# Conditioning weights of a two-block network: sums kept in SBUF, summed by transposes, and loads dealt out differently over an unrolled kernel

## The reference

```python
def modulate(h, shift, scale):
    return h * (1 + scale) + shift

def adaln(cond, w_ada, b_ada):
    return jnp.split(jax.nn.silu(cond) @ w_ada + b_ada, ADA_CHUNKS, axis=-1)   # ADA_CHUNKS = 6

# in second_block
m_lat = [m[:, None, :] for m in adaln(c, w_ada[l], b_ada[l])]
m_ctx = adaln(c_ctx, w_ada[l], b_ada[l])
hc = modulate(rms_norm(ctx, norm1_g[l]), m_ctx[0], m_ctx[1])
h = modulate(rms_norm(x, norm1_g[l]), m_lat[0], m_lat[1])
x_new = x + m_lat[2] * merge_branches(oa, ob, ga, gb, w_br_a[l], w_br_b[l], w_out[l])
x_new = swiglu_sublayer(x_new, m_lat[3], m_lat[4], m_lat[5], norm2_g[l], w_ff_gate[l], w_ff_up[l], w_ff_down[l])
```

## Time and profile before

| | |
|---|---|
| median of the runs | 3304.38 us (3300.89 to 3312.08) |
| profiled execution | span 3298.8 us from the first to the last instruction; its own time lies among the runs and is not shown apart, so what lies around the span is 5.6 us against the median and 2.1 us against the lowest run |
| PE busy | 3120.9 us, 95% |
| DVE busy | 2047.9 us, 62% |
| ACT busy | 1373.2 us, 42% |
| DMA | 580.31 MB, mean 176 GB/s |
| mean granted clock of PE | 0.972 |

### The profile page before, as it was taken

The page is one execution under the profiler, slowest core; times in us unless marked ns, Lnnn a source line. Parts: engine busy times, 40 slices in busy tenths (PEclk is TensorE's granted clock), DMA queues, the critical chain, the costliest instruction groups (busy, mean ns, idle before and its releaser), DMA issues.

```text
span 3298.8 us, 60062 instructions
## 1 busy us (share of the span) xinstructions
PE 3120.9 (95%) x24326; PEld 3017.0 (91%) x24326; DVE 2047.9 (62%) x2535; ACT 1373.2 (42%) x1565; POOL 13.5 (0%) x29
## 2 busy tenths in 40 slices
PE   7998889999999998879999988999999999999998
PEld 6888879999999998879999955999998999999998
DVE  4666877777778687763354877566655444444443
ACT  4444344444443334342223445444434444444332
POOL 1000000000000000000000000000000000000000
PEclk8999889999999999999999989999999999999999
DMA  5443757787777674622324510477754556555554
GB/s 167 136 124 127 258 161 256 259 261 265 258 254 250 220 251 131 211 77 84 88 79 137 158 44 1 165 231 230 233 169 148 183 177 188 181 184 181 183 185 141
DMA packets 300066, 580.31 MB, mean 176 GB/s; under 512 B 20560, under 2 KB 21039, under 8 KB 299151
## 3 DMA queue, kind: packets, MB, share of 16 engines
q1 hardware_dynamic: 298559, 574.09, 54.8%
q0 software_dynamic: 1360, 4.11, 0.4%
HBM read 576.04 MB, written 2.10 MB: 175 GB/s over the span
## 4 chain that ended last, share of the span: by engine, by line
PE 76%; DVE 10%; DMA 7%; issue 3%; ACT 3%; DVEq 0%; SPq 0%; ACTq 0%; POOL 0%
PE psum L483 20%; PE psum L485 19%; PE psum L486 19%; PE psum L520 3%; PE psum L524 3%; PE psum L522 3%; DVE psum L569 3%; DMA w_raw<-in_w_ffn_up 3%; DMA w_raw<-in_w_ada 2%; ACT w_hi L540 2%; PE psum L631 2%; DVE w_lo L585 2%; PE psum L1908 1%; DMA w_raw<-in_w_ple_gate 1%; PE psum L1899 1%
## 5 line engine op out<-in xcount | busy, mean ns | idle before, releaser
L585 DVE TENSOR_TENSOR w_lo<-w_raw,w_hi 128x1024 fp32r<-128x1024 f32 x888 | 1081.5, 1224 | 1040.6 <-ACT w_hi L540 1037.9
L540 ACT ACTIVATE w_hi<-w_raw 128x1024 fp32r<-128x1024 f32 x888 | 936.2, 1058 | 1567.6 <-PE psum L486 977.9
L483 PE MATMUL psum<-x_split,w_hi 128*128 128x256 f32 x4928 | 1419.0, 288 | 46.2 <-DVE x_split L672 21.6
L485 PE MATMUL psum<-x_split,w_hi 128*128 128x256 f32 x4928 | 1406.5, 285 | 0.0
L486 PE MATMUL psum<-x_split,w_lo 128*128 128x256 f32 x4928 | 1406.0, 285 | 0.0
L483 PEld LDWEIGHTS psum<-x_split,w_hi 128*128 128x128 f32 x4928 | 959.0, 195 | 57.7 <-issue 49.3
L485 PEld LDWEIGHTS psum<-x_split,w_hi 128*128 128x128 f32 x4928 | 958.9, 195 | 0.7
L486 PEld LDWEIGHTS psum<-x_split,w_lo 128*128 128x128 f32 x4928 | 958.2, 194 | 0.0
L483 PE MATMUL psum<-hidden_split,w_hi 128*128 128x256 f32 x1408 | 400.1, 284 | 4.6 <-issue 4.6
L485 PE MATMUL psum<-hidden_split,w_hi 128*128 128x256 f32 x1408 | 399.5, 284 | 0.0
L486 PE MATMUL psum<-hidden_split,w_lo 128*128 128x256 f32 x1408 | 399.4, 284 | 0.0
(11 more groups left out here) (270 smaller groups left out, 2775.3 us busy)
## 6 DMA issues: line engine op xcount, KB each, us to landing
w_raw<-in_w_in SPq DMA_DIRECT2D x216, 512.0 KB, 3.7
w_raw<-in_w_ada SPq DMA_DIRECT2D x192, 512.0 KB, 4.7
w_raw<-in_w_ffn_up SPq DMA_DIRECT2D x176, 512.0 KB, 4.8
w_raw<-in_w_ffn_down SPq DMA_DIRECT2D x88, 512.0 KB, 5.1
w_raw<-in_w_ff_gate SPq DMA_DIRECT2D x88, 512.0 KB, 3.5
w_raw<-in_w_ff_up SPq DMA_DIRECT2D x88, 512.0 KB, 4.4
w_raw<-in_w_ff_down SPq DMA_DIRECT2D x88, 512.0 KB, 3.8
w_raw<-in_w_out SPq DMA_DIRECT2D x64, 512.0 KB, 4.6
```

What stands on the lines that cost most here:

```text
L483: nc.tensor.matmul(to, hi, x_hi, start=kt == 0 and f % 2 == 0, stop=False, skip_group_check=True)
L485: nc.tensor.matmul(to, hi, x_lo, start=False, stop=False, skip_group_check=True)
L540: nc.scalar.activation(w_hi[:, b.slot(n)], raw[:, b.raw_slot(k)], ACT.Copy).then_inc(w_rounded, 1)
L585: nc.vector.tensor_tensor(w_lo[:, slot], raw[:, b.raw_slot(k)], r(w_hi[:, slot]), ALU.subtract).then_inc(w_split, 1)
```

## The change

The projection's sum stays in SBUF from the first part on (`ADA_SUM`, in the tiles `stat` and `small`); there is no copy. PE no longer multiplies by ones: it turns the sum with four transposes per condition into PSUM banks 6 and 7, and DVE sums over the free dimension with one `tensor_reduce` per condition. The PE part stands after the second unit behind the last part (`n == at + 2`), DVE's reduction one unit later.

The 192 loads are dealt over seven stages: 8 in `out`, 64 in `up`, 24 in `down`, 8 in `gate`, 48 in `branch`, 8 in `out2` and 32 in `up2`. Of the eight column groups with two conditions one stands in `out` and seven in `up`. Before, two stood in `out`, four in `down` and two in `gate`. The bias and gain of chunks 3 to 5 are applied later, before `norm2` and before `down2`.

The ring `w_raw` has six slots (`RAW = 6`), `w_hi` and `w_lo` keep four. SP may issue load k when load k-6 is done. The room for it comes from a smaller descriptor area (`dynamic_dma_scratch_size=4096`). All loops are unrolled, so `Body` and `bodies` are gone.

```diff
+RAW = 6
 PHASES = {
-    "out": Phase([8] * 4, 1, (0, 1, 23)),
-    "up": Phase([8, 8], 11, (8, 1)),
-    "down": Phase([22, 22], 2, (2, 2)),
-    "gate": Phase([8, 8], 2, (6, 1)),
-    "branch": Phase([8, 8, 8, 4], 4, (19, 1)),
-    "out2": Phase([8, 8], 2, (0, 0)),
-    "up2": Phase([8, 8], 11, (0, 0)),
...
+    "out": Phase([8] * 4, (0,)),
+    "up": Phase([8] * 22, (1, 2, 3, 4, 5, 6, 7, 12)),
+    "down": Phase([22] * 4, (13, 14, 15)),
+    "gate": Phase([8] * 4, (16,)),
+    "branch": Phase([8, 8, 8, 4] * 4, (8, 9, 10, 11, 17, 18)),
+    "out2": Phase([8] * 4, (19,)),
+    "up2": Phase([8] * 22, (20, 21, 22, 23)),
...
-        raw = sb("w_raw", [P, RING, 2, GC])
+        raw = sb("w_raw", [P, RAW, 2, GC])
...
+        def ada_turn(pe, b, n):
+            for i, at in enumerate(b.done):
+                if n == at + 2:
+                    pe.wait_ge(w_split, b.load(b.last_part[i]) + RAW + 1)
+                    pe.wait_ge(ada_evacuated, b.ada_group(i) + 1)
+                    for v in range(b.conditions(i)):
+                        for f in range(NF):
+                            ins = nc.tensor.transpose(PS[:, 6 + v, f * P:f * P + P],
+                                                      ADA_SUM[v][:, f * P:f * P + P], const("ident"))
+                    ins.then_inc(ada_turned, 1)
...
-                    for i, at in enumerate(b.ph.done):
-                        if n == at + 3:
-                            pe.wait_ge(ada_copied, b.ada(i) + 1)
-                            pe.wait_ge(ada_evacuated, b.ada(i) + 1)
-                            for v in range(ada_conditions(name, i)):
-                                for f in range(NF):
-                                    mm = nc.tensor.matmul(ADA[:, f, v:v + 1], ADA_SUM[v][:, f * P:f * P + P],
-                                                          const("ones")[:, 0:1], start=f == 0 and v == 0,
-                                                          stop=True, skip_group_check=True)
-                            mm.then_inc(ada_reduced, 1)
...
                 for v in range(nv):
-                    acc_v, c = PS[:, 6 + v, :], COND[:, 2 * u + t, v:v + 1]
+                    c = COND[:, 2 * u + t, v:v + 1]
                     if u == 0 and t == 0:
-                        ins = nc.vector.tensor_scalar(acc_v, raw[:, slot, t], c, None, ALU.mult)
+                        ins = nc.vector.tensor_scalar(ADA_SUM[v], raw[:, slot, t], c, None, ALU.mult)
                     else:
-                        ins = nc.vector.scalar_tensor_tensor(acc_v, raw[:, slot, t], c, acc_v, ALU.mult, ALU.add)
+                        ins = nc.vector.scalar_tensor_tensor(ADA_SUM[v], raw[:, slot, t], c, ADA_SUM[v],
+                                                             ALU.mult, ALU.add)
-            if u == 7:
-                dve.wait_ge(w_split, b.load(k) + RING + 1)
-                for v in range(nv):
-                    ins = nc.vector.tensor_copy(ADA_SUM[v], PS[:, 6 + v, :])
-                ins.then_inc(ada_copied, 1)
+        def ada_evac(dve, b, n):
+            for i, at in enumerate(b.done):
+                if n == at + 3:
+                    dve.wait_ge(ada_turned, b.ada_group(i) + 1)
+                    for v in range(b.conditions(i)):
+                        ins = nc.vector.tensor_reduce(MADA[:, b.ada_cols[i] * NF:(b.ada_cols[i] + 1) * NF, v],
+                                                      PS[:, 6 + v, :].rearrange("p (f n) -> p f n", f=NF),
+                                                      AX.X, ALU.add)
+                    ins.then_inc(ada_evacuated, 1)
...
-    nc = bacc.Bacc("TRN2", target_bir_lowering=False, num_devices=1)
+    nc = bacc.Bacc("TRN2", target_bir_lowering=False, num_devices=1,
+                   dynamic_dma_scratch_size=4096)
```

More of the change, by code:

```diff
@@ L156 @@
     _p.load0, _p.unit0, _p.group0, _p.ada0 = _u, _n, _g, _a
[L157 to L160, removed]
+    _u += len(_p.body)
+    _n += len(_p.units)
+    _g += len(_p.Us)
+    _a += _p.ada
 UNITS, ADA_GROUPS = _n, _a
 assert ADA_GROUPS == 6 * D // GC
[L165 to L225, removed]
@@ L228, in bodies @@
[L228 to L237, removed]
 class Chain:
     def __init__(self, eng, sem):
-        self.eng, self.sem, self.n, self.i, self.per = eng, sem, 0, None, 0
+        self.eng, self.sem, self.n = eng, sem, 0
     def mark(self, ins):
@@ L251, in wait @@
     def wait(self, n=None):
[L252 to L262, removed]
+        self.eng.wait_ge(self.sem, self.n if n is None else n)
 def build(nc, A, out, tables):
@@ new lines, in stream_pe @@
+        def stream_pe(pe, name, rhs, ready=None, first=None, late=None):
+            b = PHASES[name]
+            for n, (j, u) in enumerate(b.units):
+                slot = b.slot(n)
+                if u == 0:
+                    pe.wait_ge(evacuated, b.group(j) + 1)
+                    if first is not None:
+                        first(j)
+                if ready is not None and j == 0 and u % 2 == 0:
+                    ready(u // 2)
+                pe.wait_ge(w_split, b.load(b.at[n]) + RAW + 1)
+                for t in range(2):
+                    kt = 2 * u + t
+                    last = kt == 2 * b.Us[j] - 1
+                    for f in range(NF):
+                        hi = w_hi[:, slot, t, f * P:f * P + P]
+                        lo = w_lo[:, slot, t, f * P:f * P + P]
+                        to = accf(b.set(j), f)
+                        x_hi, x_lo = rhs(j, kt)
+                        nc.tensor.matmul(to, hi, x_hi, start=kt == 0 and f % 2 == 0, stop=False,
+                                         skip_group_check=True)
+                        nc.tensor.matmul(to, hi, x_lo, start=False, stop=False, skip_group_check=True)
+                        mm = nc.tensor.matmul(to, lo, x_hi, start=False, stop=last, skip_group_check=True)
+                mm.then_inc(w_used, 1)
+                ada_turn(pe, b, n)
+                if late is not None:
+                    late(b, j, u)
@@ new lines, in stream_act @@
+        def stream_act(act, name, evac, late=None, evac_first=False):
+            b = PHASES[name]
+            for n, (j, u) in enumerate(b.units):
+                if evac_first and u == b.Us[j] - 1:
+                    evac(b, j, n)
+                if not b.is_last(n):
+                    k = b.ahead(n)
+                    act.wait_ge(w_landed[b.raw_slot(k)], b.landed(k))
+                    act.wait_ge(w_used, b.unit(n) + RING + 1)
+                    nc.scalar.activation(w_hi[:, b.slot(n)], raw[:, b.raw_slot(k)],
+                                         ACT.Copy).then_inc(w_rounded, 1)
+                if not evac_first and u == b.Us[j] - 1:
+                    evac(b, j, n)
+                if late is not None:
+                    late(b, j, u)
@@ L777, in stream @@
             def stream(name):
[L778 to L784 removed]
+                b = PHASES[name]
+                for k, x in enumerate(b.body):
+                    if name == "in" and k == RAW:
+                        sp.dma_start(WDT, W_IN[:, :, 2560:2592]).then_inc(S("wdt_landed"), 16)
+                    slot = b.raw_slot(k)
+                    sp.wait_ge(w_split, b.load(k) + 1)
+                    sp.dma_start(raw[:, slot], source(name, x)).then_inc(w_landed[slot], 16)
             stream("in")
```

314 lines of the change are left out of this document (142 added, 172 removed).

## The result

The changed kernel takes 3233.96 us (median of 4 runs, 3232.68 to 3235.07) against 3305.85 for the kernel before on the same chip (4 runs). The ratio is 0.9773, 95% interval 0.9753 to 0.9792. The profiled execution's span fell from 3298.8 to 3232.3 us, by 66.5; the forecast had 65.8 and a time of 3239.

| stage | before | forecast | after |
|---|---|---|---|
| `out` | 114.3 | 93.3 | 93.1 |
| `up` | 534.2 | 525.2 | 521.8 |
| `down` | 267.8 | 254.8 | 254.7 |
| `gate` | 119.6 | 95.1 | 94.3 |
| `branch` | 326.3 | 325.6 | 325.3 |

The account below looks back on a forecast made before the run. PE at 2.88 us a unit was taken as the floor, with only some 95 us of stage excess winnable. Terms summing to -65.8 us on a span of 3298.8, plus 5.6 around it, gave 3239, range 3224 to 3264.

Parts of the forecast that it names:

- The sum: Whole kernel: the stage terms add to -65.8 us on a span of 3298.8, giving 3233.0; with 5.6 around it, 3238.6.
- `out` and `gate`: Stages with fewer two-condition parts: DVE no longer holds PE up; `out` -20.9 us to 93.3, `gate` -24.5 to 95.1.
- `down`: Stage `down`: unrolling removes a 7.0 us stop and restart at the second pass, cheaper sections follow; -13.1 us to 254.8.
- `up`: Stage `up`: eleven sections and their waits go, transposes and two new waits with low clock come; -8.9 us to 525.2.
- The two long waits: In `up`, beside units 0 of column groups 8 and 16: PE waits 2.6 us for DVE's last part, twice.
- The ring: Six load slots in `w_raw`: costed at nothing; without their lead `branch` would take up to 5 us more.
- DVE's price with the sum in SBUF: DVE's parts of the projection: no change from 752 ns an operation; the skill's figures would make it 65 ns cheaper.
- A: Rival: DVE bounds `up`, busy 454.7 us; `up` takes 22 us more, some 3260 in all; chance 0.12.
- B: Rival: unrolled code arrives late at PE, 7.0 us each time; fifteen such stops give 3344; chance 0.03.
- C: Rival: loads bound `branch` at 256 GB/s, +5 us there, 3244 in all; chance 0.12.
- D: Rival: transposes let the clock fall, 2.4 us at each of 24 sections, +58 us, 3297; chance 0.04.
- E: Rival: better than forecast, no waits in `up` at (8,0) and (16,0) nor their low clock, -9.6 us, 3228; chance 0.13.

Follow-up runs that it names:

- the second profile: The changed kernel run once more with nothing altered, on the same chip as the other follow-up runs: 3230.64 us, span 3229.2.

## Why the prediction was right, and where it was not

**The sum** is nearer than its parts. The stages gained 70.0 us where the forecast had 65.8, and some 3 us of that were lost again in the stretch between `gate` and `kv`, at a lower granted clock. The change is no reason for it: with four slots, or the transposes one unit later, the same dealing has 43.8 us there, and over all profiles it is 43.6 to 48.1, at clocks of 0.91 to 0.79. The agreement of the spans to 0.7 us is luck to that extent. The time is 4.6 us below the forecast's 3238.6, mostly by "what lies around the span". I took 5.6 us, the distance of one profile's span to the median of other executions. In every run on record 1.7 to 2.2 us lie between an execution's time and its own span.

**`out` and `gate`** (-20.9 and -24.5 forecast, -21.2 and -25.3 measured). The mechanism held: DVE had too much for PE's 2.88 us a unit. With four slots and the new summing the dealing takes `out` from 115.5 to 93.2 us by itself, and `gate` from 110.1 to 95.1. It is not the only cure, though: with the old dealing the loop, the summing and the ring already bring `gate` to 105.2, and `out` to 108.2.

**`down`** (-13.1 forecast and measured). Written out alone it gave 7.2 for the jump, forecast 7.0. The sections gave the rest: 256.9 with the old dealing and transposes, 254.7 with the new.

**`up`** (-8.9 forecast, -12.4 measured). This is the step whose reasons failed. "There unrolling wins nothing" is wrong: it is -13.7, and what goes with the loop is 21 table loads of 1.28 us. The trace accounts for it at the eleven sections: with their waits they take 10.2 us in place of 19.8, and the slow matmuls behind three of them, some 4 us, are gone. The sum came out since I removed the waits of 8.2 us and their slow clock as part of the sections; they went, but through the loop. From 520.5 on, the new summing with four slots gives nothing (522.5, with 6.6 us of waits), the six slots take 8.4 (514.1), and the dealing then costs 5 to 8. The two long waits were forecast at 2.6 us; one was 2.26, the other 1.23. My 7.36 us behind the boundary came from a row with a table load in it, which may be why; that the two places differ was not looked into. The slow clock behind both, 3.6 us in the sum, was some 1.5 in all, and 0.1 in the second profile with the same two waits: a term of luck.

**The ring** was "costed at nothing". With the new dealing that is right, and the alternative of 5 us in `branch` did not occur. But the reason, that `up` had its rate "without a wait on a load", is wrong, and with the old dealing the same term would have been 20 us. I looked at PE's waits and not at ACT's. In `up` of the kernel before they read:

```profile
ACT w_hi L540 <- DMA w_raw<-in_w_ffn_up: 178.1, 100, 4.9
```

**DVE's price with the sum in SBUF** held at 749 ns against 752, so the 65 ns an operation, the estimate that the prediction took from the Trainium skill's "VectorE: DVE Perf Modes" (the section on the TRN2 errata), do not show. That section prices PSUM to SBUF, and here the sum also went back to PSUM. The first part of a group did get cheaper: 481 against some 747 ns. The Trainium skill's "VectorE: DVE Perf Modes" ("The perf-mode tier table") has `tensor_scalar` in fp32 at double rate from SBUF, and says under "Why PSUM operands drop a tier" that a PSUM operand takes it away; the rows agree.

**The rivals.** A: DVE is busy 438.8 of 521.9 us in `up`, forecast 454.7; not bound. B: 190 instruction packets for 110, and no stop for code inside a stage. C: no; `branch` has one wait of ACT for a load, of 2.0 us, and 325.3 us. D: no loss of clock behind transposes, four, eight or (doubled) sixteen. E came about in part, with `up` 3.4 us below the forecast: the two waits stayed, at 3.5 us for 5.2, and less slow clock stood behind them. (Its -9.6 should read -9.0 by the forecast's own terms.)

**The floor.** "2.88 us a unit is the floor that this change leaves alone" is true of the change. It is no floor of the kernel: 2.80 us is to be had by moving one tile.

## What to carry to other kernels

When parts of a change cure the same lateness (here ring, dealing, loop and place of the sum), price them by a table of combinations, for a right total doesn't show which one did it. A wait that ends on the engine that bounds the kernel often starts two engines up: follow it from PE to DVE to ACT, and read the waits and table loads there. Where nothing waits for the engine between, as in `up2`, the same table loads cost nothing. And when every instruction of a kind is slower than it has to be by the same few per cent, look at addresses before schedules.

## What the runs showed of the hardware

- The interval between fp32r matmuls of 256 columns depends on where stationary and moving operand lie in SBUF: 120 ns (253.4 us for 2112) with both at a multiple of 64 bytes or both 32 bytes past one, 116.7 ns (246.4 us) with the stationary one at a multiple of 64 and the moving one 32 past. Over the kernel 69 us. Only these three placements were run; whether 64 is the step that matters, what the opposite placement does, and why it is so, stays open.
- In a loop whose ACT body uses a function of another table, ACT paid two table loads of 1.28 us a pass, though written out the same stream needs one in all (22 against 1, in `up` and in `up2`).
- Four fp32 matmuls by a column of ones are eight records and cost as much as eight transposes of 128 x 128 (0.81 and 0.79 us).
- The granted clock of one and the same stretch of work, that between `gate` and `kv`, lay anywhere from 0.79 to 0.91 over the profiles, and its length from 48.1 to 43.6 us. Spans of single profiles can differ by as much without a cause in the change; the two profiles of the changed kernel differ by 3.
